# Where the first RMS norm is applied in a two-block Trainium2 kernel

## What is computed

```
def rms_norm(x, g):
    y = xf * lax.rsqrt(jnp.mean(xf * xf, axis=-1, keepdims=True) + EPS)
    return (y * g)

def gla_mixer(h, w_in, w_gk_up, b_gk, g_onorm, w_out):       # h = rms_norm(x, norm_mix)
    proj = h @ w_in
    q, k, v, r, gk_low = jnp.split(proj, ...)                # widths 512, 512, 1024, 1024, 16
    log_a = jax.nn.log_sigmoid(gk_low @ w_gk_up + b_gk) / GLA_GATE_NORM
    ...                                                      # per head: decays exp(+-cumsum(log_a)), chunked attention
    o = rms_norm(o, g_onorm)
    return (o * jax.nn.silu(r)) @ w_out
...
x = x + mixer(rms_norm(x, norm_mix)); x = x + sqrelu_mlp(rms_norm(x, norm_ffn), w1, w2)
```

## Time and profile before

| | us |
|---|---|
| median of the timed runs | 1641.07 |
| the profiled execution's own time | 1639.36 |
| its span, first to last instruction | 1637.5 |
| PE busy in the span | 1583.8 (97%) |
| DVE busy | 1128.2 (69%) |
| ACT busy | 799.9 (49%) |
| from the start to the first small product of head 0 | 65.88 |
| one head, from its first small product to the next head's | 46.1 to 46.5 |

### The profile page before, as it was taken

How to read it: one execution, slowest core, us unless ns; L and a number is a source line. 1 busy time by engine, 2 the same in 40 slices (tenths; PEclk the granted TensorE clock), 3 DMA queues, 4 the chain that set the end, 5 groups by cost and what they waited for, 6 DMA issues and landing times.

```text
span 1637.5 us, 24024 instructions
## 1 busy us (share of the span) xinstructions
PE 1583.8 (97%) x9298; PEld 1267.7 (77%) x9298; DVE 1128.2 (69%) x1709; ACT 799.9 (49%) x1230; POOL 222.3 (14%) x206
## 2 busy tenths in 40 slices
PE   6999989999999999999999999999999999999999
PEld 3777767888888887667667887878888888888887
DVE  5555544595959597788676758576685468686868
ACT  6455553644444456334554435363463373636353
POOL 0233340000000001233310501305031000000000
PEclk8999999999999999999999999999999999999999
DMA  4222212524241412223203123121320361414131
GB/s 149 78 65 66 78 39 77 193 66 139 62 144 57 143 33 84 65 64 90 54 1 103 53 67 89 41 78 41 82 73 14 93 204 64 141 65 141 65 103 52
DMA packets 197856, 135.85 MB, mean 83 GB/s; under 512 B 10667, under 2 KB 185276, under 8 KB 197748
## 3 DMA queue, kind: packets, MB, share of 16 engines
q1 hardware_dynamic: 197748, 134.36, 27.4%
HBM read 132.16 MB, written 2.18 MB: 82 GB/s over the span
## 4 chain that ended last, share of the span: by engine, by line
PE 78%; DVE 9%; issue 7%; ACT 4%; POOL 1%; DMA 1%; SPq 0%; PEldq 0%; ACTq 0%; POOLq 0%; DVEq 0%; PEld 0%
PE bank L241 11%; PE bank L243 11%; PE bank L242 11%; PE bank L997 6%; PE bank L998 6%; PE bank L999 6%; PE bank L505 4%; PE bank L2004 4%; PE bank L507 3%; PE bank L506 3%; DVE arena L2308 2%; DVE w_lo L225 1%; ACT w_hi L221 1%; PE bank L1829 1%; PE bank L1558 1%
## 5 line engine op out<-in xcount | busy, mean ns | idle before, releaser
L225 DVE TENSOR_TENSOR w_lo<-raw,w_hi 128x1024 fp32r<-128x1024 f32 x154 | 192.9, 1253 | 97.7 <-ACT w_hi L221 97.1
L241 PE MATMUL bank<-m_hi,w_hi 128*128 128x512 f32 x592 | 233.8, 395 | 4.4 <-POOL w_lo L231 2.8
L243 PE MATMUL bank<-m_hi,w_lo 128*128 128x512 f32 x592 | 230.7, 390 | 0.0
L242 PE MATMUL bank<-m_lo,w_hi 128*128 128x512 f32 x592 | 230.5, 389 | 0.0
L221 ACT CAST w_hi<-raw 128x1024 fp32r<-128x1024 f32 x170 | 177.5, 1044 | 87.7 <-PE bank L243 55.4
L1029 ACT CAST d_hi<-arena 128x1024 fp32r<-128x1024 f32 x112 | 117.9, 1053 | 130.7 <-PE bank L999 130.7
L241 PE MATMUL bank<-h_hi,w_hi 128*128 128x512 f32 x368 | 148.0, 402 | 9.0 <-DVE h_lo L376 4.7
L243 PE MATMUL bank<-h_hi,w_lo 128*128 128x512 f32 x368 | 145.3, 395 | 0.0
L242 PE MATMUL bank<-h_lo,w_hi 128*128 128x512 f32 x368 | 145.2, 395 | 0.0
L1034 DVE TENSOR_TENSOR d_lo<-arena,d_hi 128x1024 fp32r<-128x1024 f32 x112 | 136.1, 1220 | 10.9 <-ACT d_hi L1029 10.8
L241 PEld LDWEIGHTS bank<-m_hi,w_hi 128*128 128x128 f32 x592 | 111.1, 188 | 30.6 <-POOL w_lo L231 3.2
(11 more groups left out here) (327 smaller groups left out, 3332.8 us busy)
## 6 DMA issues: line engine op xcount, KB each, us to landing
raw<-in_w_in SPq DMA_DIRECT2D x64, 512.0 KB, 3.8
raw<-in_l_w_ff SPq DMA_DIRECT2D x32, 512.0 KB, 4.1
arena<-in_l_w_ff SPq DMA_DIRECT2D x32, 512.0 KB, 5.7
raw<-in_w_mlp_up SPq DMA_DIRECT2D x32, 512.0 KB, 4.1
arena<-in_w_mlp_down SPq DMA_DIRECT2D x32, 512.0 KB, 5.5
raw<-in_l_w_in SPq DMA_DIRECT2D x24, 512.0 KB, 3.8
raw<-in_l_w_out SPq DMA_DIRECT2D x8, 512.0 KB, 4.1
arena<-gb_rows SPq DMA_DIRECT2D x16, 256.0 KB, 4.9
```

Of the source, the lines that this page charges most:

```text
L225: dve.tensor_tensor(w_lo[q.par][:], raw[q.par][:], w_hi[q.par][:].bitcast(F32), ALU.subtract).then_inc(s["w_ready"], 1)
L241: pe.matmul(g_bank[q.par][:], w_hi[q.par][:, k], hi[:, k], start=(k == 0), stop=False)
L242: pe.matmul(g_bank[q.par][:], w_hi[q.par][:, k], lo[:, k], start=False, stop=False)
L243: last = pe.matmul(g_bank[q.par][:], w_lo[q.par][:, k], hi[:, k], start=False, stop=(k == KT - 1))
```

## The change

The first mixer takes x times its gain, without the factor r_0. So the tiles `h_hi` and `h_lo` are made from the transposed x in PSUM as soon as it is turned: one ACT instruction that scales by the gain and casts (`high`), one DVE instruction (`low`). Every result of those products is multiplied by r_0 afterwards, on DVE, when its bank is emptied (`evac`, and L614 of the new code for `gk_low`). r_0 is made from squares of the untransposed x, summed along the free axis by ACT's accumulator (`squares`), spread by DVE, turned by PE (`pe_norm`) and kept in `g_rep`, which therefore gets its own content only ahead of the MLP. The gate panel has 16 columns instead of 128 (`pe_rank`); the panels q and k stand partly ahead of the gates; the fence is gone; the masks are loaded later. The work of head 0's gates comes first on ACT and DVE, the rest between panels. The division by 16 is in the scale of the exponentials. In the heads DVE empties all panels; tanh reads SBUF and stands behind an exponential (`gate`), and the product with the gate is a second DVE instruction (`gated`).

In the diff "..." marks what is left out.

```
+    sp.dma_start(ident[:], const_square[:, 0:P]).then_inc(s["x_in"], 16)
+    x_piece(0)
+    gain(*gain_rows[0], "mix_in")
+    load(sp, Panel(N_GK, 0, 0, 0), [(rows(t["l0_w_in"])[:, :, GLA_G0:GLA_G0 + GLA_RANK], 0)])
+    x_piece(1)
+    x_piece(2)
+    load(sp, N_Q0, [(rows(t["l0_w_in"])[:, :, GLA_Q0:GLA_Q0 + P], 0)])
+    x_piece(3)
+    for row in gain_rows[1:]:
+        gain(*row, "params_in")
     sp.dma_start(par_rows[0:CONV * 24, 1, :],
                  t["conv_w_2"].rearrange("a j (c p) -> (a j c) p", p=P)).then_inc(s["params_in"], 16)
...
-    load(sp, Panel(N_GK, 0, 0, 0), [(rows(t["l0_w_in"])[:, :, GLA_G0:GLA_G0 + 16], 0),
-                                    (rows(t["l0_w_in"])[:, :, 0:P - 16], 16)])
+
...
-    sp.dma_start(g_rep[:], t["final_norm"].rearrange("(o d) -> o d", o=1).broadcast_to([P, D])).then_inc(s["g_in"], 16)
-
-PARAM_DMAS = 11
+
+PARAM_DMAS = 10
...
+def pe_rank(pe, k):
+
...
+    pe.wait_ge(s["h_ready"], k + 1)
+    o = g_bank[q.par][0:GLA_RANK, :]
+    left, left_lo = w_hi[q.par][:, k, 0:GLA_RANK], w_lo[q.par][:, k, 0:GLA_RANK]
+    pe.matmul(o, left, h_hi[:, k], start=(k == 0), stop=False)
+    pe.matmul(o, left, h_lo[:, k], start=False, stop=False)
+    last = pe.matmul(o, left_lo, h_hi[:, k], start=False, stop=(k == KT - 1))
...
+    def turn(k):
         if k in (2, 4, 6):
             pe.wait_ge(s[f"x_in{k // 2}"], 16)
-        if k >= 2:
-            pe.wait_ge(s["x_s"], k - 1)
+        if k == 5:
+            pe.wait_ge(s["par_s"], 1)
+        if k >= 6:
+            pe.wait_ge(s["x_s"], k - 5)
         for tt in range(TT):
-            last = pe.transpose(b[k % 2][:, tt * P:(tt + 1) * P], x_tok[:, tt, k * P:(k + 1) * P], ident[:])
+            last = pe.transpose(b[k % 6][:, tt * P:(tt + 1) * P], x_tok[:, tt, k * P:(k + 1) * P], ident[:])
         last.then_inc(s["x_t"], 1)
+
+    turn(0)
+    pe.wait_ge(s["mix_in"], 16)
+    pe.transpose(b[5][:, 0:KT], par_rows[0:KT, 0, :], ident[0:KT, 0:KT]).then_inc(s["par_t"], 1)
...
+    for k in range(1, 4):
+        turn(k)
+    pe_rank(pe, 0)
+    pe_rank(pe, 1)
+    turn(4)
+    turn(5)
+    for k in range(2, 6):
+        pe_rank(pe, k)
+    turn(6)
+    turn(7)
+    for k in range(4):
+        pe_eighth(pe, N_Q0, k)
+    pe_rank(pe, 6)
+    pe_rank(pe, 7)
+    for k in range(4, KT):
+        pe_eighth(pe, N_Q0, k)
     pe.wait_ge(s["params_in"], 16 * PARAM_DMAS)
+    pe.wait_ge(s["x_s"], 4)
...
-    for k in range(KT):
+    act.wait_ge(s["par_t"], 1)
+    act.copy(gains[:, 0:KT], b[5][:, 0:KT]).then_inc(s["par_s"], 1)
+    q = Panel(N_GK, 0, 0, 0)
+    act.wait_ge(raw_in[q.par], 16)
+    act.wait_ge(mm_done[q.par], 1)
+    act.copy(w_hi[q.par][:, :, 0:GLA_RANK], raw[q.par][:, :, 0:GLA_RANK]).then_inc(s["w_hi_ready"], 1)
+    act.wait_ge(s["par_s"], 1)
+
...
+    def high(k):
         act.wait_ge(s["x_t"], k + 1)
-        act.copy(x[:, k], b[k % 2][:]).then_inc(s["x_s"], 1)
-        act.wait_ge(s["x_s"], k + 1)
-        if k >= 2:
-            act.wait_ge(s["n_acc"], k - 1)
-        act.activation(x_sq[:, k % 2], x[:, k], ACT.Square).then_inc(s["n_sq"], 1)
-    act.wait_ge(s["par_t"], 1)
-    act.copy(gains[:], b[2][:, 0:N_GAIN]).then_inc(s["par_s"], 1)
+        act.activation(h_hi[:, k], b[k % 6][:], ACT.Copy, scale=gains[:, k:k + 1]).then_inc(s["n_hi"], 1)
+
+    def squares(j, tt):
+        c = slice(j * SEQ, (j + 1) * SEQ)
+        act.activation(x_junk[:, tt, c], x_tok[:, tt, c], ACT.Square, accum_out=sq_cols[:, j, tt:tt + 1]
+                       ).then_inc(s["n_sq"], 1)
+
+    def keep_x(k):
+        act.wait_ge(s["h_ready"], k + 1)
+        act.copy(x[:, k], b[k % 6][:]).then_inc(s["x_a"], 1)
+
...
+    for k in range(4):
+        high(k)
+    act.wait_ge(s["x_in1"], 16)
+    for tt in range(TT):
+        squares(0, tt)
+    high(4)
+    high(5)
+    act_split(act, N_Q0)
+    high(6)
+    high(7)
+    act.wait_ge(s["x_in3"], 16)
+    squares(1, 0)
+    squares(1, 1)
+    act_split(act, N_Q0.next())
+    squares(1, 2)
+    squares(1, 3)
+    keep_x(4)
+    act.wait_ge(s["n_t"], 1)
+    act.wait_ge(s["memsets"], 2)
+    act.activation(r_col, sq_sum, ACT.Ln, scale=1.0 / D, bias=eps[:]).then_inc(s["n_ln"], 1)
+    act.wait_ge(s["n_ln"], 1)
+    act.activation(r_col, r_col, ACT.Exp, scale=-0.5).then_inc(s["n_r"], 1)
     act.wait_ge(s["par_t"], 2)
+    act.copy(gains[:, KT:N_GAIN], b[2][:, KT:N_GAIN]).then_inc(s["par_s"], 1)
+    act.wait_ge(s["par_t"], 3)
     act.copy(conv_w[:], b[3][:, 0:CONV * 24]).then_inc(s["par_s"], 1)
+    act_split(act, Panel(N_GLA, 12, 0, 2))
+    for k in range(5, KT):
+        keep_x(k)
+    act.wait_ge(s["n_ss"], 1)
+    act.copy(r_0, b[4][:]).then_inc(s["n_r0"], 1)
...
     def low(k):
         dve.wait_ge(s["n_hi"], k + 1)
-        dve.tensor_tensor(h_lo[:, k], hb[:, k % 2], h_hi[:, k].bitcast(F32), ALU.subtract).then_inc(s["h_ready"], 1)
-
+        dve.scalar_tensor_tensor(h_lo[:, k], b[k % 6][:], gains[:, k:k + 1], h_hi[:, k].bitcast(F32),
+                                 ALU.mult, ALU.subtract).then_inc(s["h_ready"], 1)
+
+    def keep_x(k):
+        dve.tensor_copy(x[:, k], b[k][:]).then_inc(s["x_s"], 1)
+
...
+    low(0)
+    low(1)
+    keep_x(0)
+    keep_x(1)
+    low(2)
+    low(3)
+    keep_x(2)
+    keep_x(3)
+    low(4)
+    low(5)
+    dve_split(dve, N_Q0)
+    low(6)
+    low(7)
+    dve_split(dve, N_Q0.next())
+    dve.wait_ge(mm_done[q.par], 2)
+    dve.tensor_copy(gk_low[0:GLA_RANK, :], g_bank[q.par][0:GLA_RANK, :]).then_inc(s["gkl"], 1)
+    dve.wait_ge(s["gkl"], 1)
+    dve.sem_inc(bank_free[q.par], 1)
+    dve.wait_ge(s["n_sq"], 2 * TT)
+    dve.tensor_tensor(sq_sum, sq_cols[:, 0], sq_cols[:, 1], ALU.add).then_inc(s["n_t"], 1)
     dve.wait_ge(s["n_r"], 1)
-    for k in range(KT):
...
+    dve.tensor_copy(tiles(r_wide), r_col.unsqueeze(2).broadcast_to([P, TT, P])).then_inc(s["n_bc"], 1)
+    dve.wait_ge(s["par_s"], 3)
+
+    dve.tensor_scalar(gains[:, G_ON:G_ON + 3], gains[:, G_ON:G_ON + 3], 0.5, None, ALU.mult).then_inc(s["memsets"], 1)
+    dve_split(dve, Panel(N_GLA, 12, 0, 2))
...
 def pe_norm(pe):
-    pe.wait_ge(s["memsets"], 2)
...
+    pe.wait_ge(s["n_bc"], 1)
+    pe.wait_ge(s["x_a"], 1)
+    for tt in range(TT):
+        last = pe.matmul(b[4][:, tt * P:(tt + 1) * P], r_wide[:, tt * P:(tt + 1) * P], ident[:], start=True, stop=True)
+    last.then_inc(s["n_ss"], 1)
...
 def sp_gla(sp):
-    sp.wait_ge(s["phase_done"], 4)
+    sp.dma_start(gk_up[0:GLA_RANK, :], t["l0_w_gk_up"]).then_inc(s["gk_in"], 16)
     sp.dma_start(keep, const_wide[4]).then_inc(s["gk_in"], 16)
-    sp.dma_start(gk_up[0:GLA_RANK, :], t["l0_w_gk_up"]).then_inc(s["gk_in"], 16)
     w = rows(t["l0_w_in"])
-    with sp.Fori(0, GLA_H) as h:
...
+            if u >= first:
+                load(sp, Panel(N_GLA, 6, h, u), [(w[:, :, bass.ds(c, P)], 0)])
+            if first and u == 1:
+                sp_consts(sp)
+
+    head(0, 1)
+    with sp.Fori(1, GLA_H) as h:
+        head(h, 0)
...
 def pe_gates(pe):
-    pe_panel(pe, Panel(N_GK, 0, 0, 0), h_hi, h_lo, s["h_ready"], 0)
+    q = N_Q0.next()
+    pe_eighth(pe, q, 0)
+    pe_eighth(pe, q, 1)
+    pe_norm(pe)
+    for k in range(2, 6):
+        pe_eighth(pe, q, k)
     pe.wait_ge(s["gk_in"], 32)
-    pe.wait_ge(s["gkl"], 1)
+    pe.wait_ge(s["gkl"], 2)
+    pe.wait_ge(s["par_s"], 3)
+    pe.wait_ge(s["x_a"], 4)
     for h in range(GLA_H):
         pe.matmul(b[h][:], gk_up[0:GLA_RANK, h * P:(h + 1) * P], gk_low[0:GLA_RANK, :],
                   start=True, stop=True).then_inc(s["gk_ps"], 1)
+    pe_eighth(pe, q, 6)
+    pe_eighth(pe, q, 7)
...
+    act.wait_ge(s["par_s"], 2)
+    sizes(0)
+    sizes(1)
+    logs(0)
+    act_split(act, Panel(N_GLA, 12, 0, 3))
+    logs(1)
+    sizes(2)
+    sizes(3)
+    logs(2)
+    logs(3)
+    act_split(act, Panel(N_GLA, 12, 0, 4))
...
-        dve.wait_ge(s["gscan"], h + 1)
-        dve.tensor_scalar(b_all[:, h], b_all[:, h], 1.0 / GLA_GATE_NORM, None, ALU.mult).then_inc(s["gbs"], 1)
...
+    dve.wait_ge(s["n_r0"], 1)
+    dve.tensor_tensor(gk_low[0:GLA_RANK, :], gk_low[0:GLA_RANK, :], r_0[0:GLA_RANK, :], ALU.mult).then_inc(s["gkl"], 1)
+    evac(0, 0, 0, N_Q0)
+    dve.wait_ge(s["gk_in"], 32)
+    least(0)
+    least(1)
+    sums(0)
+    evac(0, 0, 1, Panel(N_GLA, 12, 0, 1))
+    dve_split(dve, Panel(N_GLA, 12, 0, 3))
+    sums(1)
+    dve.wait_ge(s["gscan"], 2)
+    exponent(0, 0)
+    exponent(0, 1)
+    evac(0, 0, 2, Panel(N_GLA, 12, 0, 2))
+    dve_split(dve, Panel(N_GLA, 12, 0, 4))
+    least(2)
+    least(3)
+    sums(2)
+    sums(3)
+    evac(0, 0, 3, Panel(N_GLA, 12, 0, 3))
     dve.sem_inc(s["gla_done"], 1)
...
-    def q_evac(g, e, u, q):
...
-            act.mul(dst[:, 0], g_bank[q.par][:], GLA_K ** -0.5).then_inc(s["q_in"], 1)
...
-        else:
-            act.activation(dst[:, u], g_bank[q.par][:], ACT.Tanh, scale=0.5).then_inc(s["tg"], 1)
+    def gate(g, e, u):
+        act.wait_ge(s["z_in"], 2 * g + u - 3)
+        act.activation(tgate[:, u - 4], head_in[e][:, u], ACT.Tanh, scale=0.5).then_inc(s["tg"], 1)
```

(43 more changed lines are left out.)

153 lines of the change are left out of this document (50 added, 103 removed).

## The result

The changed kernel took 1626.43 us in the median of four runs (1625.40 to 1627.24), the kernel before 1641.27: a ratio of 0.9909 (0.9891 to 0.9926), 14.8 us less where 17.2 were forecast. A second series gave 1628.87 (1626.96 to 1631.98) against 1641.97, 0.9926 (0.9912 to 0.9941).

A forecast was written before the change was run, and what follows sets the result against it. Up to 52 us a chain of waits through norm and gates bounds the kernel, then PE in the heads. 16.6 us (start) plus 0.6 (last head) off 1639.36, with 1.71 added for the median, gave 1623.9 us; range 1618 to 1631.

The forecast's parts named there:

- The start: Everything up to head 0's first small product: forecast at 49.3 us against 65.88, 16.6 us less.
- the list of work: PE's panels, gate products and smaller products from the last turn of x to head 0, together 28.1 us.
- The 1.0 us for r_0 and the bank: Allowance before head 0 for r_0 coming late and panel k waiting on its bank: 1.0 us.
- the near tie: Before the gate products: `gk_low` ready at 29.8 us, PE done with six eighths of k at 29.6.
- The clock term: Granted clock lost before head 0: 1.6 us behind the gate products plus 1.2 for thin products, 2.8 together.
- The 1.2 us for the thin products before 17 us: Clock lost through thin products at the start, before 17 us: 1.2 us, between 0 and 3.6.
- I cost this at nothing: In the heads, four more DVE instructions each, 2.8 us, taken as covered by PE's products: no cost.
- Rival two: The heads become DVE's: all its added work is on the path, 9.8 us, 1633.7 us; chance 0.06.
- 0.6 us less: Last head: tanh behind the exponential brings the cast about 0.6 us sooner; gain 0.6 us, 0 to 2.
- The level-5 wait: Last head: the level-5 small product's wait for POOL, 2.65 us before, was to be shorter.
- the marks I had set for being wrong: Head 0 later than 55 us, a head over 47 us, or span and head 0 start differences over 2 us apart.
- Rivals three and four: Three: clock stays lower from turns to head 0, 1649.2 us, 0.04; four: everything behind gates waits as before, 1632.4, 0.05.

The follow-up runs named there:

- e7: e1 with the four products that turn the norm factor moved from behind the second to behind the sixth eighth of panel k on PE: 1627.37 us.
- after: The changed kernel itself, as against the kernel before: 1626.43 us, ratio 0.9909.
- e9: e1 with the exponent of level 6 moved ahead of the split it followed on VectorE: 1619.20 us, ratio to the kernel before 0.9869.
- e1: The changed kernel with both `gated` products of a head moved behind the three state updates on VectorE: 1621.24 us, ratio to the kernel before 0.9889.
- e5: e1 with each tanh of the gate behind both exponentials of its pair on ScalarE, not between them: 1622.81 us.
- e11: The changed kernel itself, unaltered, measured again in a second series: 1628.87 us, ratio to the kernel before 0.9926.
- e3: The changed kernel with the `gated` products reading the bank of the head's transposed values instead of z in SBUF: 1622.94 us.
- e4: The changed kernel with q and k panels in the heads emptied by ScalarE again, without r_0 for heads 1 to 3: 1626.35 us.
- e6: e1 with an eighth of panel k between the first and second, and second and third, of the four 16-row gate products: 1623.49 us.
- e12: e1 with the gate products of heads 2 and 3 moved behind the first v panel: 1624.58 us.

## Why the prediction was right, and where only in the sum

**The start** was right in its mechanism and in its order. Panel q began at 16.61 (forecast 17.4), next to the turns, without a wait. From there it was 28.9 us to head 0, where the list of work said 28.1. The 1.0 us for r_0 and the bank was not needed: r_0 and `gk_low` were done at 28.7, the eighth ahead of the gates at 29.3. 0.6 us of slack is what the near tie had left; e7 shows what lay behind it.

**The clock term**, 2.8 us, was the size of something that either comes or doesn't: 0 in after's first profile (head 0 at 45.52) and 3.2 in the second (48.72, forecast 49.3). Sized from the earlier trace rows at 1.6 for the gates, it is twice that where it comes. The 1.2 us for the thin products before 17 us was wrong: 1.00 in every stretch from 5 to 30 us in all profiles.

**"I cost this at nothing"** is the step that failed. Heads 0 to 2 gave back 4.5 us. I had looked for PE waiting on VectorE directly and found none; PE waits for GpSimd, and GpSimd for VectorE. I had priced `gated` at 0.69 us, from a row that reads one operand from a bank; with two SBUF operands beside GpSimd it takes 1.21 and delays the exponent by as much. Rival two said "the exponents stand behind the new instructions", which was the place, but charged all four instructions (9.8 us); q and k cost next to nothing (e9), and of `gated` it is not the load (e1).

**"0.6 us less" in the last head** failed with the wrong sign: 2.9 us more in the first profile, 1.1 in the second. The cast came forward by 0.24 us, not 0.6 (e5), and `gated` stands between it and the exponent. The level-5 wait, forecast to be shorter, went from 2.65 to 2.88 us. Two of the marks I had set for being wrong were met, a head over 47 us and spans that differ by 7.3 us less than the starts of head 0.

So the time fell inside the range partly by luck, since two errors had opposite signs: the start 3.8 us better than forecast, the heads and the last stretch 7.9 worse; together that is the profiled 1626.35 instead of 1622.2. In the second profile the start was only 0.6 better. A third error was on the good side: the median was put 1.71 above the profiled execution and lay 0.08 above it. Rivals three and four did not happen: no stretch from the turns to 30 us ran below full clock, and panel k stood ahead of head 0 as the list said.

## What to carry to other kernels

Price a moved instruction by a row in which the same neighbours run, not by its kind alone: with two SBUF operands beside GpSimd's own, 0.68 us became 1.21, and GpSimd's 0.73 became 1.72 beside a split. Follow a wait through two engines before calling an engine off the path. An instruction that nobody waits for soon belongs where the other engine is idle; here that one move, and an exponent set ahead of a split, took 7.0 us off the heads and the last stretch (e9 against e11).

## What was not expected of the hardware

- A VectorE instruction with one operand in a bank ran at its full 0.68 us beside GpSimd (e3, eight of eight between 675 and 678 ns), and spared the next one, which reads two SBUF operands, its wait.
- The granted clock fell behind the 16-row gate products in four of twelve profiles with r_0 on time (e4, e6, e9, e11), with PE at 5.00 of 5 us busy; head 0 came 3 to 6 us later. Panel work between the products (e6) did not keep it from happening; with half of them moved (e12) the one profile does not show it, though it lies 3.9 us above the fastest run. What decides it from one execution to the next stays open. A wait of 1.43 us ahead of the products brought it in the one profile that has it (e7).
